# Wide rank products, two-tile first units and re-ordered edges in a one-core fp32 transformer kernel

## What is computed

```
for i in range(2):                                   # first block
    h = rmsnorm(x, g_mix[i]); u = h @ w_in[i]
    sb_q, sb_k, sb_v, da_q, da_k, da_v, gate_a, gate_b = split(u)
    y_a = stick_breaking_attention(sb_q, sb_k, sb_v) @ w_br_a[i]
    y_b = rmsnorm(differential_attention(rope(da_q), rope(da_k), da_v, lam), g_subln[i]) * c
    merged = sigmoid(gate_a) * y_a + sigmoid(gate_b) * (y_b @ w_br_b[i])
    x = x + merged @ w_o[i]
    t = rmsnorm(x, g_ffn[i])
    logits = t @ w_router_group[i], t @ w_router_expert[i]
    # the best of 4 groups, in it 2 of 8 experts; tokens sorted by expert, blocks of rows:
    x = x + sum(gate * (silu(t @ w_gate[e]) * (t @ w_up[e])) @ w_down[e])
    x = x + (p[i] @ w_ple[i]) * sigmoid(rmsnorm(x, g_ple[i]) @ w_ple_gate[i])
x = rmsnorm(x, g_final)
h = x + 0.5 * rms_norm(swiglu(rms_norm(x, ffn1_pre_g)), ffn1_post_g)      # "ffn0" in the kernel
cq, ckv, kr, dq, dk, dv, g = split(rms_norm(h, mix_pre_g) @ w_in_2)
merged = sigmoid(g_0) * (latent_attention(cq, ckv, kr) @ w_branch_a)
       + sigmoid(g_1) * (dilated_attention(rope(dq), rope(dk), dv) @ w_branch_b)
h = h + rms_norm(merged @ w_out, mix_post_g)
h = h + 0.5 * rms_norm(swiglu(rms_norm(h, ffn2_pre_g)), ffn2_post_g)      # "ffn1" in the kernel
```

## Time and profile before

| | us |
|---|---|
| runs of the kernel before | 3192.29, 3195.6, 3203.16 |
| their median | 3195.6 |
| the profiled execution | 3196.94 |
| its span in the trace | 3195.2 |
| TensorE busy | 3007.1 (94%) |
| mean granted clock of TensorE | 0.972 of full |
| VectorE, GpSimd, ScalarE busy | 1323.8, 829.4, 619.5 |
| moved by DMA | 412.75 MB, mean 129 GB/s |

### The profile page before, as it was taken

How to read it: one execution, slowest core, us unless ns; L and a number is a source line. 1 busy time by engine, 2 the same in 40 slices (tenths; PEclk the granted TensorE clock), 3 DMA queues, 4 the chain that set the end, 5 groups by cost and what they waited for, 6 DMA issues and landing times. The chain is left out here.

```text
span 3195.2 us, 31434 instructions
## 1 busy us (share of the span) xinstructions
PE 3007.1 (94%) x12384; PEld 1875.5 (59%) x12384; DVE 1323.8 (41%) x2188; ACT 619.5 (19%) x1009; POOL 829.4 (26%) x637
## 2 busy tenths in 40 slices
PE   8999998999899999989997999998999999799996
PEld 6854464333368544643333588885654345588885
DVE  4346543111343465431223644434444464544432
ACT  2033222111210233221112300002112341300000
POOL 5200022222132000123221154543300001345443
PEclk9999999999899999989998999998999999899998
DMA  4211123999522111149996122221211111122220
GB/s 180 79 53 40 53 86 134 387 388 386 205 79 79 53 40 53 66 142 359 381 374 258 66 93 79 93 93 66 92 72 40 66 40 53 60 86 93 79 93 27
DMA packets 80914, 412.75 MB, mean 129 GB/s; under 512 B 25792, under 2 KB 25920, under 8 KB 34176
## 3 DMA queue, kind: packets, MB, share of 16 engines
q1 hardware_dynamic: 56144, 387.67, 32.1%
q0 software_dynamic: 24624, 23.08, 2.2%
HBM read 513.41 MB, written 31.46 MB: 171 GB/s over the span
## 5 line engine op out<-in xcount | busy, mean ns | idle before, releaser
L2699 POOL TENSOR_TENSOR ATT<-ring 128x512 f32<-128x512 f32 (+1 forms) x95 | 122.4, 1289 | 1195.1 <-PE PS L956 731.4
L956 PE MATMUL PS<-G,ring 128*128 128x256 f32 x1312 | 310.3, 379 | 0.0
L956 PE MATMUL PS<-HT,ring 128*128 128x256 f32 x1216 | 283.7, 386 | 25.9 <-ACT HT L2251 15.3
L956 PE MATMUL PS<-G,ATT 128*128 128x256 f32 x1184 | 280.0, 379 | 0.0
L956 PEld LDWEIGHTS PS<-HT,ring 128*128 128x128 f32 x1216 | 234.8, 194 | 65.4 <-issue 15.4
L956 PEld LDWEIGHTS PS<-G,ring 128*128 128x128 f32 x1312 | 249.3, 190 | 33.9
L956 PEld LDWEIGHTS PS<-G,ATT 128*128 128x128 f32 x1184 | 225.0, 190 | 31.9 <-issue 1.4
L2443 ACT ACTIVATE TMP<-PS 128x256 f32<-128x256 f32 x89 | 34.2, 384 | 1059.5 <-PE PS L956 939.9
L899 PE MATMUL PS<-ring,G 128*64 128x512 f32 x1024 | 229.6, 601 | 0.0
L523 PE MATMUL PS<-HT,ring 128*128 128x512 f32 x448 | 205.1, 600 | 3.8 <-DVE G L1402 3.8
L1853 DVE TENSOR_TENSOR BIG<-PS,TMP 128x256 f32<-128x256 f32 x100 | 42.4, 424 | 359.1 <-ACT TMP L2443 357.1
(11 more groups left out here) (340 smaller groups left out, 4449.3 us busy)
## 6 DMA issues: line engine op xcount, KB each, us to landing
ring<-in_stream SPq DMA_DIRECT2D x164, 1024.0 KB, 4.8
ring<-in_experts_gu SPq DMA_DIRECT2D x128, 1024.0 KB, 8.7
ring<-in_experts_down SPq DMA_DIRECT2D x64, 1024.0 KB, 8.9
G<-expert_rows SPq DMA_DIRECT2D x8, 1024.0 KB, 8.0
h_tokens<-G POOLq DMA_DIRECT2D x2, 2048.0 KB, 7.4
XT<-in_xT SPq DMA_DIRECT2D x2, 1024.0 KB, 7.8
G<-in_pT POOLq DMA_DIRECT2D x2, 512.0 KB, 6.3
out_T<-XT SPq DMA_DIRECT2D x2, 512.0 KB, 3.6
```

The costliest lines, as they stand in the source:

```text
L956: mm = pe.matmul(product(g, name), x[:, k * P:(k + 1) * P], y[:, k, :], start=first and k == 0 and name in ("P1", "P2", "P3", "P5"), stop= ...
L2699: pool.tensor_tensor(a["S1"], a["A21"], a["A22"], ALU.add)\
```

## The change

It has no switch; these parts come together:

1. `first_unit`: in both layers and in the mixer, for each raw tile k both output tiles get their matmul. The norm's sums move behind: in the layers into the second unit, in the mixer behind the third matmul of the next unit, whose tile now uses bank 5.
2. ffn1's first unit is plain, by the same `two_tiles`; GpSimd leaves its weight sums out, VectorE and ScalarE take the two tiles directly; the norm moves ahead of P3 of unit 1.
3. ScalarE stores raw tiles 5, 6 and 7 ahead of their squares at the ends of both layers; in both ffns' last units the two squares come ahead of the two scalings.
4. Six of the router's eight matmuls move between the last two output-projection tiles.
5. The rank takes five matmuls: the triangle over all four tiles at once, then for each tile t one product by ones whose right-hand side is repeated over the tiles behind it.
6. GpSimd's second memset goes; ScalarE writes zeros in two activations. `TABLE_AT` is 4. `gate_up(0)` stands ahead of `turn_x(1)`.
7. Stick-breaking: one sigmoid, the query's rotation, then the other sigmoids. The last differential branch tile moves behind the norm's four products.
8. `gate_fill` gives a whole gate tile to every even step and none to an odd one; VectorE takes it behind the step's rotation.

```
+            def two_tiles(block, banks, rhs):
+                for k in range(KD):
+                    pe.wait_ge(Q["raw_ready"], now.next("raw_ready"))
+                    mm = [pe.matmul(banks[m], block(m, k), rhs[:, k, :], start=k == 0, stop=k == KD - 1)
+                          for m in range(2)]
+                return mm
...
-                        if i == 0 and name == "P5" and f == 1:
-                            norm_sum(KD, 7)
+                        if i == 1 and name == "P3" and f == 1:
+                            norm_sum(KD, 3)
...
                     if j:
-                        for k in range(SB_GATE[j - 1], SB_GATE[j]):
+                        next_sigmoid()
+                    rope([DAQ[:, j, :]], COS, SIN)
+                    if j:
+                        for k in range(SB_GATE[j - 1] + 1, SB_GATE[j]):
                             next_sigmoid()
-                    rope([DAQ[:, j, :]], COS, SIN)
...
-                for m in range(len(DA_BRANCH), KD):
+                for m in range(len(DA_BRANCH), KD - 1):
                     project_tile(a, 4, 512, SBQ, m)
...
+                project_tile(a, 4, 512, SBQ, KD - 1)
...
-                project(unit(), KD, 256, src, "lin_ready")
+                units = {}
+                for m in range(2):
+                    project_tile(units, KD, 256, src, m)
+                    if m == 0:
+                        between()
...
-                first = True
+                pe.matmul(PS[:, 5, 0:TT * NE], BEFORE, ATT[:, 0:TT * NE], start=True, stop=False, skip_group_check=True)
                 for t in range(TT):
-                    for s in range(t + 1):
-                        mm = pe.matmul(PS[:, 5, t * NE:(t + 1) * NE], BEFORE if s == t else ONES, M[:, s, :],
-                                       start=first, stop=s == t, skip_group_check=True)
-                        first = False
-                for t in range(TT):
-                    mm = pe.matmul(PS[:, 5, TT * NE:(TT + 1) * NE], ONES, M[:, t, :],
+                    mm = pe.matmul(PS[:, 5, (t + 1) * NE:(TT + 1) * NE].rearrange("p (t x) -> p t x", x=NE), ONES,
+                                   M[:, t, :].unsqueeze(1).to_broadcast([P, TT - t, NE]),
                                    start=False, stop=t == TT - 1, skip_group_check=True)
...
                 turn_x(0)
+                gate_up(0)
                 turn_x(1)
-                gate_up(0)
...
-                project_half(gates, HT, u)
+                if u % 2 == 0:
+                    project_tile(gates, KD, 256, HT, u // 2)
...
-            store_scaled(CQ, 3)
+            store_scaled(CQ, 3, spare=2)
...
-                if u % 2:
-                    take_gate(u // 2, scaled=True)
                 if u in DIL_ROPES:
                     rope([(DQ, DK)[DIL_ROPES.index(u) % 2][:, 1 + DIL_ROPES.index(u) // 2, :]], COS, SIN)
+                if u % 2 == 0:
+                    take_gate(u // 2, scaled=True)
...
+                        for i in range(2):
+                            act.activation(BIGF[:, i * 4 * S:(i + 1) * 4 * S], ONES[:, 0:1].to_broadcast([P, 4 * S]),
+                                           ACT.Identity, scale=0.0).then_inc(Q["rx_zeroed"], now.inc("rx_zeroed"))
...
-                pool.memset(BIGF[:, 0:8 * S], 0.0).then_inc(Q["tails_zeroed"], now.inc("tails_zeroed"))
```

More of the change, by code:

```diff
@@ L547, in new_item, with sums_of @@
                 return u
+            def sums_of(u):
+                return u + 1 - ("ffn1" in at and u > at["ffn1"][0])
             def item_done(u):
@@ L606, in quartered_tokens, with router, output_projection @@
                 item_done(u)
-            def output_projection(name, src):
+            def router(L, k0, k1):
+                if k0 == 0:
+                    pe.wait_ge(Q["const_landed"], N_CONST)
+                    pe.wait_ge(Q["tile_done"], 2 * len(at["groups"]))
+                for k in range(k0, k1):
+                    pe.wait_ge(Q["raw_ready"], now.next("raw_ready"))
+                    mm = pe.matmul(PS[0:NG + NE, 4, :], WR[:, L, k, :], RX[:, k, :], start=k == 0, stop=k == KD - 1)
+                if k1 == KD:
+                    mm.then_inc(Q["lg_rows"], now.inc("lg_rows"))
+            def output_projection(name, src, between=lambda: None):
                 t0, taken = next_sums(4), now.count("lin_ready")
@@ L805, in moe @@
             def moe(L):
[L807 to L812, removed]
+                router(L, 6, KD)
                 norm_sum(KD)
@@ L974, in ffn @@
                     u, g = new_item([st["unit"]]), new_group(None if i else 0)
-                    if i == 1:
+                    if f == 1 and i == 0:
+                        a = weight_blocks(w, u, 4)
+                        a = [[a["A11"], a["A12"]], [a["A21"], a["A22"]]]
+                        mm = two_tiles(lambda m, k: a[m][k // 4][:, k % 4 * P:(k % 4 + 1) * P], [PS[:, 0, :], PS[:, 1, :]],
+                                       HT)[-1]
+                        mm.then_inc(Q["unit_done"], now.inc("unit_done"))
+                        unit_used("unit_done")
+                        item_done(u)
+                        at["groups"][g]["done"] = now.count("unit_done")
+                        continue
+                    if i == 1 + f:
                         drained("gate_ready")
@@ L1064, in _ @@
                 branch(DAQ)
-                output_projection(f"out{L}", HT)
+                output_projection(f"out{L}", HT, lambda: router(L, 0, 6))
                 moe(L)
@@ L1894, in ffn @@
                 for i in range(0, KF, 2):
-                    quarter_sums(g0 + i, GATED)
-                    by_rstd(GATED, "gate_scaled")
+                    if f == 1 and i == 0:
+                        v.wait_ge(Q["unit_done"], at["groups"][g0]["done"])
+                        for m in range(2):
+                            v.wait_ge(*now.prev())
+                            v.tensor_tensor(GATED[:, m * S:(m + 1) * S], PS[:, m, :], RSTD[:, :], ALU.mult)\
+                                .then_inc(Q["tile_done"], now.inc("tile_done"))
+                    else:
+                        quarter_sums(g0 + i, GATED)
+                        by_rstd(GATED, "gate_scaled")
                     hid = BIGF[:, i * S:(i + 2) * S]
@@ L2487, in _ @@
                 if L:
-                    for k in range(KD - 2, KD):
-                        mix_input(k)
                     layer_roots()
@@ L2547, in _ @@
                         now.skip("gate_free")
-                    if k >= 2:
+                    done = range(5, KD) if k == KD - 1 else range(max(k - 2, 0), k - 1)
+                    for n in done:
+                        tile_added(n)
                         if L == LAYERS - 1:
-                            final_input(k - 2)
+                            final_raw(n)
                         else:
-                            mix_input(k - 2)
+                            raw_tile(n, "g_mix1")
+                    for n in done:
+                        if L == LAYERS - 1:
+                            final_squares(n)
+                        else:
+                            square(XT)
                 act.preload_act_table_set("natural_log_exp_and_others")
-            for k in range(KD - 2, KD):
-                final_input(k)
             st["norm"] += 1
```

117 lines of the change are left out of this document (60 added, 57 removed).

## The result

The changed kernel takes 3202.76 us (median of 20 runs, 3197.17 to 3205.36), the kernel before 3195.36 (20 runs, 3190.82 to 3203.16). The ratio is 1.0019, with a 95% interval of 1.0013 to 1.0026: slower, by 6 us after the ratio and 7.4 after the two medians. The forecast was 3192.9, so the time lies in the range, but the move has the other sign. It stays within the 0.3% that I called no measurable change; with 20 runs each it could be told.

What follows compares the result with a forecast made beforehand. TensorE was taken as the bound nearly everywhere, with only its idle time, half-speed stretches and removable work to win. Gains against dilated attention's +32.3 and the branch's +1.2 summed to -4.0, from 3196.94 to 3192.9 us; range 3178 to 3213.

Steps and rivals of the forecast that it cites:

- Dilated attention, the chain of waits: Mixer's attention: odd turns wait for VectorE's maxima and normalising, 13 gaps of 2.02 us; with smaller terms +26.6 us.
- Dilated attention, the clock: Same attention: half clock costs +4.2 us behind two gaps of about 4.2 and 1.5 for the 2.0 us gaps.
- Stick-breaking: Both layers: rotating the query after one sigmoid shortens waits and removes layer 1's clock loss, -4.9 us.
- Last branch tile: Differential attention's end, both layers: the branch starts 0.6 us later per layer, +1.2 us.
- Expert entry: Mixture-of-experts entry, both layers: fewer rank matmuls, no slow copy, earlier slot table and turn_hidden(0), -9.7 us.
- ffn1's first unit: Start of ffn1: 16 plain matmuls starting with the first tile finish earlier than 28 quartered ones, -9.5 us.
- the mixer's first unit: Mixer's start: the second tile's matmuls fill three waits and a half clock goes, -7.3 us.
- ffn0's entry and the ends: Raw stores first shorten ffn0's third product's wait, -3.3 us; squares back to back at both ffns' ends, -2.6 us.
- C: Rival: the thirteen 2.0 us gaps in dilated attention halve the clock, about 2.2 us each, up to 3220; chance 0.10.
- A: Rival: every entry reaches its better bound and no further clock is lost, 3180.8 us; chance 0.15.
- B: Rival: VectorE's maxima are not held by the turn, so dilated attention costs nothing, 3158 us; chance 0.06.
- D: Rival: the entries give back half to ScalarE's and VectorE's chains, +13, 3210 us; chance 0.13.

Runs made afterwards that it cites:

- e1: Changed kernel with the dilated attention's gate tiles again in halves, one at every step: 3161.97 us, ratio to before 0.9892.
- e2: Kernel before with only the whole gate tile at even steps of the dilated attention: 3239.08 us, ratio 1.0140.
- e3: Changed kernel, but at odd steps of the dilated attention VectorE normalises step u before taking the maxima of u+1: 3175.01 us.
- e4: Changed kernel with two more 128x512 multiplications by 1.0 ahead of the normalising at odd steps, lengthening the waits: 3224.61 us.
- e8: e1 with VectorE's old stick-breaking order, all sigmoids ahead of the query's rotation: 3162.50 us.
- e12: e1 with last branch tile before the norm's products, router in one piece, block 0's gate before turned block 1's copy, sigmoids before rotation: 3152.35 us.
- e10: e1 with the last differential branch tile again ahead of the norm's products: 3158.85 us.
- e5: e1 with the old expert entry (router in one piece, 14 rank matmuls, GpSimd's memset, old table place and turn order): 3171.67 us.
- e6: e1 with ffn1's first unit quartered again, its norm in it and its weight sums on GpSimd: 3171.56 us.

## Why the prediction was wrong, step by step

- *The bound* was read rightly: each part acted through TensorE's idle time and clock, and where another engine or a transfer entered it was by when it ended, not by its share of busy time.
- *Dilated attention, the chain of waits*: right in mechanism, place and size (idle +26.1, forecast +26.6), by e1, e2 and e3; the count of 13 should have been 12, which the small new waits made up for.
- *Dilated attention, the clock*: the step that failed. "A gap of 2.0 us lies nearer to the first", with 1.5 us for all of them, was 6.8: four of twelve such gaps had a half clock behind them, in the changed kernel and in e2. I had read the price of 1.60 us (none of five) as a step, where e4 has ten of twelve at 2.88. Nor were the five all that there was: the trace of before has a gap of 1.75 us ahead of 1387.92 with a half clock from 1388.4 on, and one of 1.61 and one of 1.62, each beside another wait, with a half clock close by. "The two longer gaps [...] halved the clock in this trace, for about 2.1 us each" was 2.6 to 2.7 each; the trace of before had no such gap of 4.2 us, and its 3.20, 3.21 and 3.58 lost 1.4 to 2.8. The ends of rows, 1.9 us, were not in the sum at all. With +39 the sum would have been +2.7 and its sign right.
- *Stick-breaking*: -4.9 was -0.5 by e8 and -2.4 by e12. Of its 3.8 us of idle 1.7 came, since the changed order moves more of the wait on to the values than I had taken; its 1.1 from the clock rested on a dip that one execution had and another has not.
- *Last branch tile*: sign right, +1.2 forecast, 2.0 between the traces and 3.1 by e10; the same gap grew from 3.2 to 4.2, and I had priced 0.6 and no clock.
- *Expert entry, ffn1's first unit, the mixer's first unit*: -9.7, -9.5 and -7.3 against 9.7, 9.6 and 7.0 in runs of their own. These chains had been followed row by row to the instruction that comes last. The entry's sum is closer than its halves: between the traces the two layers gained 3.0 and 6.2 (4.5 and 5.2 forecast), and single runs scatter by several us, so agreement to 0.1 us is partly luck.
- *ffn0's entry and the ends*: -4.6 between the traces against -3.3 and -1.3 for those of ffn0; not run alone. The third product's wait fell from 6.24 to 1.79, and the norm behind it now waits 1.99 for the last square, as forecast.
- *Rivals*: C was the one that happened, in part: by four gaps of the six from which I let it decide, and with the two long gaps costing somewhat more. The Trainium skill, "TensorE: Matmul & The Clock Gate", section "A second HAM failure mode: psum-queue depth-cycling", spoke for it. The trace agrees that frequent short idles make the clock swing, but a third of such gaps cost, where I had taken that rule to mean all. A, B and D did not happen; B's mechanism is what e3 builds by hand.

The parts run alone make up 9.7 + 9.6 + 7.0 + 0.5 - 3.1 = 23.7 of e1's 34.6 us. Between the traces ffn0 adds 4.6. Some 6 us are left to the start, the passage between the layers and the ends, for which I had 1.5 in the sum; whether that is their worth or the clock's chance is open.

## What to carry to other kernels

Work that covers a softmax must stand between each pair of dependent turns; grouped into every second one it covers half of them, even if its sum is the same. Ask of every gap in the tensor engine's stream what it costs in clock, too: in this attention each one of about 2 us cost its own length and, one time in three, 1.7 us more. Where input tiles arrive one by one, a plain product that starts on the first beats one with fewer multiplications that needs half of them.

## What the runs showed of the hardware

I had not expected that the clock's price comes in equal portions. In the dilated attention every half clock behind a gap of about 1.96 us took 1.7 us. Around all 22 gaps of 4.2 us in the traces of these kernels the clock fell, for 3.4 us of clock in 19 of them and for 1.7 in three (one each in e5, e6 and e8); what of it falls into the gap itself costs nothing.

Nor had I expected how much it is chance for one and the same gap: 1.96 us ahead of a turn did at 2364 and not at 2376 of the same execution, and at the start of layer 0 the 2.74 us of the kernel before did while the 3.17 of the changed one did not. What decides is open, and length alone does not: over all traces the clock fell behind 13 of the 16 gaps of 2.10 ahead of turn_hidden(0), but behind only 7 of the 16 of 2.57 in the stick-breaking. A clock dip read in one trace is no term for a sum; its frequency over like gaps at the same place is.
